# Moving transposes, one block of modulation sums and the first folds of the last norm in a one-core diffusion-layer kernel

## The reference

```python
ada = silu(cond) @ w_ada + b_ada            # six 1024-wide vectors per group
sh1, sc1, g1, sh2, sc2, g2 = split(ada, 6)
h = modulate(layer_norm(x), sh1, sc1)
proj = h @ w_in                             # pooling input, q, k, v, o, gates
pool_out = pool_mixer(proj[..., :512])
ml_out, state = mlstm_mixer(q, k, v, o, gates)   # conv + silu on q,k; chunked scan both ways
mix = concat([pool_out, ml_out]) @ w_out
x = layer_norm(ALPHA * x + g1 * mix, ln1_g, ln1_b)
h = modulate(layer_norm(x), sh2, sc2)
up = h @ w_up; a, g = split(up, 2)          # 2 x 2816 wide
ffn = (gelu(dwconv3x3(g) + b_dw) * a) @ w_down
x = layer_norm(ALPHA * x + g2 * ffn, ln2_g, ln2_b)
```

## Time and profile before

| what | us |
|---|---|
| median of 3 runs | 1347.56 (1346.4 to 1351.62) |
| the profiled execution | 1355.02 |
| its span on the core | 1353.3 |
| PE busy | 1272.9 |
| DVE busy | 1027.4 |
| POOL busy | 668.6 |
| ACT busy | 590.7 |

### The profile page before, as it was taken

The page is one execution under the profiler, slowest core; times in us unless marked ns, Lnnn a source line. Parts: engine busy times, 40 slices in busy tenths (PEclk is TensorE's granted clock), DMA queues, the critical chain, the costliest instruction groups (busy, mean ns, idle before and its releaser), DMA issues.

```text
span 1353.3 us, 21780 instructions
## 1 busy us (share of the span) xinstructions
PE 1272.9 (94%) x7739; PEld 1176.0 (87%) x7739; DVE 1027.4 (76%) x1510; ACT 590.7 (44%) x1023; POOL 668.6 (49%) x505
## 2 busy tenths in 40 slices
PE   5899999989998898998999999999999999999995
PEld 3689999989997776888899999999999988888884
DVE  7565559984567678779988778877785689888698
ACT  5442224345345725445444444544443456345420
POOL 1000999643243111217978888797877874200011
PEclk9899999998999998999999999999999999999998
DMA  9522331473335432111534363535443579946674
GB/s 338 155 78 79 90 88 47 123 234 86 91 104 188 147 120 93 63 63 31 164 131 173 121 205 128 185 117 186 164 152 112 194 249 340 359 138 194 236 258 190
DMA packets 164851, 210.28 MB, mean 155 GB/s; under 512 B 10567, under 2 KB 102819, under 8 KB 164515
## 3 DMA queue, kind: packets, MB, share of 16 engines
q1 hardware_dynamic: 164286, 204.47, 45.7%
q0 software_dynamic: 288, 4.72, 0.9%
q10 hardware_dynamic: 197, 0.06, 0.0%
HBM read 161.49 MB, written 47.72 MB: 155 GB/s over the span
## 4 chain that ended last, share of the span: by engine, by line
PE 79%; DVE 10%; DMA 3%; ACT 3%; issue 3%; POOL 3%; SPq 0%; DVEq 0%; ACTq 0%; POOLq 0%
PE ps L1233 12%; PE ps L1582 11%; PE ps L1580 11%; PE ps L1581 11%; PE ps L1613 5%; PE ps L1614 5%; PE ps L1615 5%; PE ps L1185 2%; PE ps L1456 2%; PE ps L1458 2%; PE ps L1457 2%; DMA adaw<-in_w_ada 2%; DVE qk L2703 1%; PE ps L1511 1%; DVE aacc_side L2723 1%
## 5 line engine op out<-in xcount | busy, mean ns | idle before, releaser
L3038 DVE SCALAR_TENSOR_TENSOR ps<-gs,taps,ps 128x945 f32<-128x945 f32 (+2 forms) x176 | 215.9, 1227 | 57.1 <-ACT ps L1996 51.6
L2361 POOL TENSOR_TENSOR rstd<-mv,neghalf 128x1 f32<-128x1 f32 x27 | 26.0, 963 | 268.5 <-DVE mv L3206 161.5
L1233 PE MATMUL ps<-h1hi,whi 128*128 128x384 f32 x432 | 154.7, 358 | 4.1 <-DVE wlo L2558 3.0
L1233 PE MATMUL ps<-h1hi,wlo 128*128 128x384 f32 x432 | 146.9, 340 | 0.0
L1233 PE MATMUL ps<-h1lo,whi 128*128 128x384 f32 x432 | 146.9, 340 | 0.0
L1613 PE MATMUL ps<-dwhi,uhi 128*128 128x512 f32 x290 | 113.1, 390 | 1.3 <-POOL dwlo L2218 1.3
L1615 PE MATMUL ps<-dwhi,ulo 128*128 128x512 f32 x290 | 112.9, 389 | 0.0
L1614 PE MATMUL ps<-dwlo,uhi 128*128 128x512 f32 x290 | 112.8, 389 | 0.0
L2218 POOL TENSOR_TENSOR wlo<-raw,whi 128x512 fp32r<-128x512 f32 x46 | 68.0, 1480 | 72.7 <-ACT whi L1685 34.5
L1580 PE MATMUL ps<-thi,xhi 128*128 128x288 f32 x320 | 95.0, 297 | 3.3 <-POOL xlo L2218 3.1
L1582 PE MATMUL ps<-thi,xlo 128*128 128x288 f32 x320 | 95.0, 297 | 0.0
(11 more groups left out here) (430 smaller groups left out, 4007.7 us busy)
## 6 DMA issues: line engine op xcount, KB each, us to landing
raw<-in_w_up SPq DMA_DIRECT2D x78, 256.0 KB, 3.9
u_rows<-val SPq DMA_DIRECT2D x22, 576.0 KB, 2.9
adaw<-in_w_ada SPq DMA_DIRECT2D x24, 512.0 KB, 4.1
st<-in_w_down SPq DMA_DIRECT2D x22, 512.0 KB, 4.3
t_rows<-st SPq DMA_DIRECT2D x11, 1024.0 KB, 5.0
raw<-in_w_in SPq DMA_DIRECT2D x40, 256.0 KB, 4.4
w_raw<-in_w_down SPq DMA_DIRECT2D x33, 256.0 KB, 4.6
v_raw<-u_rows SPq DMA_DIRECT2D x33, 256.0 KB, 4.5
```

Of the source, the lines that this page charges most:

```text
L1233: last = mm(ps[:, bank, 0:GN], a[:, n % 2, k * P:(k + 1) * P], b[:, kk, grp(g)], start=(kk == 0 and a is whi and b is h1hi), stop=(kk == K ...
L3038: step(stt(a3[:, ro, co], g3[:, ri, ci], taps[:, tap:tap + 1], a3[:, ro, co], ALU.mult, ALU.add), 2 + m)
```

## The change

The change has four parts. (1) One of the eight first blocks of `w_ada` is loaded ahead of the first two projection weights. (2) One `ada_unit` moves from unit 23 to unit 30; `ada2_cols(5)` leaves unit 31 and stands behind the first matmul group of o-unit 33, directly ahead of the scores; on DVE the last `conv` stands ahead of `ada_evac`. (3) `y_at` has other slots: the transposes of tiles 0, 1, 2, 3, 4, 5, 6 stand at (3,7), (3,13), (4,10), (5,9), (6,8), (7,7), (8,5) in place of (3,12), (4,1), (4,5), (5,5), (6,5), (7,5), (8,5). (4) `N_TAIL` goes from 4 to 8. The second half rows of the last norm are no longer summed first and then gated, scaled and added: `ahead(i)`, in `D_S4` and the start of `D_S3`, gates the partial sum that is there and adds the residual; `fold(i)` gates the missing term, adds it and takes the statistics. The four loads of residual rows for indices 5 to 8 move from `D_U4` to `D_S4` and `D_S3`, and ACT's copies of the `D_S3` banks stand behind unit 6 and not unit 4.

```diff
 KD = KF * 7
 ARING = 4
 N_POOL_LO = 4
-N_TAIL = 4
+N_TAIL = 8
 N_SPLIT = 8
 UX = UC + P
 
@@ -94,7 +94,7 @@
 
 ADA_FIRST = 8
 ADA_UNITS = {4: 2, 6: 2, 7: 1, 8: 1, 9: 2, 10: 1, 11: 1, 12: 1, 13: 1, 14: 1, 15: 1, 16: 1, 17: 1, 18: 1, 19: 1, 21: 2,
-             23: 2, 24: 3, 25: 3, 26: 3, 27: 3, 28: 3, 29: 3}
+             23: 1, 24: 3, 25: 3, 26: 3, 27: 3, 28: 3, 29: 3, 30: 1}
 ADA_SIDE = (3, 5)
 
 
@@ -716,11 +716,11 @@
 
             for t in range(NT):
                 load_x0(t)
-            for i in range(3):
+            for i in range(4):
                 load_ada1(i)
             load_proj(0)
             load_proj(1)
-            for i in range(3, N_LOAD1):
+            for i in range(4, N_LOAD1):
                 load_ada1(i)
             load_proj(2)
             load_proj(3)
@@ -1019,6 +1019,10 @@
             def load_z(i):
                 sp.dma_start(zt[(i - 1) % 4 if i else 4][:, :], x1_rows[TILE_OF[i]]
                              ).then_inc(y_in[(i - 1) % 4] if i else ln_in, 16)
+
+            def load_z_again(i):
+                sp.wait_ge(z_added, ZA_0 + i)
+                load_z(H + i)
 
             def store_y(i):
                 t = TILE_OF[i]
@@ -1070,8 +1074,12 @@
                 load_d(D_S4, j)
                 if j == 5:
                     store_y(0)
+                if j in (6, 8, 10):
+                    load_z_again(j // 2 - 2)
             for j in range(N_SPLIT):
                 load_w(D_S3, j)
+                if j == 1:
+                    load_z_again(4)
                 if j < KF - N_SPLIT:
                     load_w(D_S3, N_SPLIT + j)
                 elif j < KF - N_SPLIT + ARING:
@@ -1083,10 +1091,6 @@
                     load_u(D_U4, j + ARING)
                 if 3 <= j < 3 + KF - N_SPLIT:
                     load_w(D_U4, N_SPLIT + j - 3)
-                if j in (2, 4, 6, 8):
-                    i = j // 2
-                    sp.wait_ge(z_added, ZA_0 + i)
-                    load_z(4 + i)
             for i in range(1, NT - 1):
                 store_y(i)
             for half in range(2):
@@ -1315,6 +1319,7 @@
                 o_unit(U_C, g)
             o_groups = [(n, g) for n in range(U_C + 1, U_OUT) for g in range(NG)]
             o_unit(*o_groups.pop(0))
+            ada2_cols(N_ADA2 - 1)
 
             def scores(s, d):
                 ck = scan_chunks(s)[d]
@@ -1485,7 +1490,7 @@
                     pe.wait_ge(hT_used, NT)
                     pe.wait_ge(n_ready, 1)
                     gate_bcast(1, 6)
-            y_at = {(3, 12): 0, (4, 1): 1, **{(i, 5): i - 2 for i in range(4, NT)}}
+            y_at = {(3, 7): 0, (3, 13): 1, (4, 10): 2, (5, 9): 3, (6, 8): 4, (7, 7): 5, (8, 5): 6}
             for i in range(2, NT):
                 if i == 2:
                     pe.wait_ge(growT_ready, 1)
@@ -2074,7 +2079,7 @@
                 else:
                     act.wait_ge(pe_unit, U_DOWN + KF * (p + 1))
                 if p == D_S3:
-                    act.wait_ge(down_used, 2 + i + 1)
+                    act.wait_ge(down_used, 6 + i + 1)
                 fn(z[i][:, UC:DM] if p == D_S1 else z[i][:, 0:UC], ps[:, BANKS[SET[p]][i], :], ACT.Copy).then_inc(p_copied, 1)
 
             def t_split(b, n):
@@ -2200,7 +2205,7 @@
             for j in range(KF):
                 both_hi(D_S3, j)
             for j in range(KF):
-                if j == 4:
+                if j == 6:
                     for i in range(H):
                         copy_at_end(D_S3, i)
                 both_hi(D_U4, j)
@@ -2761,10 +2766,10 @@
                     ada_unit(unit)
                 if n % 2 == 0 and n // 2 > 2 * H:
                     conv(n // 2 - 1 - 2 * H)
+            conv(2 * H - 1)
             dve.wait_ge(pe_ada, N_ADA1 + N_ADA2)
             link(ada_evac(6, A_G1, A_G2))
             tsc(ada1p[:, 1, :, :], adaT[:, A_SC2:A_SC2 + KT, :], 1.0, None, ALU.add).then_inc(ada_b, 1)
-            conv(2 * H - 1)
             dve.wait_ge(pool_y, 4)
             v.tensor_copy(Cs[:, :, :, P:P + 1], colv[:, V_N:V_N + 2 * H].rearrange("p (d h n) -> p d h n", d=2, n=1)
                           ).then_inc(cs_n, 1)
@@ -3160,16 +3165,33 @@
                 dve.wait_ge(p_copied, PC_0 + 2 + i + 1)
                 tt(z[H + i][:, 0:UC], z[i][:, 0:UC], ps[:, BANKS[1][i], :], ALU.add).then_inc(down_used, 1)
 
-            def c12(i):
-                dve.wait_ge(pe_unit, U_DOWN + KF * (D_S4 + 1))
-                dve.wait_ge(p_copied, PC_0 + 8 + i + 1)
-                out = z[H + i][:, UC:DM]
-                tt(out, out, ps[:, BANKS[1][i], :], ALU.add).then_inc(down_used, 1)
-
-            def c22(i):
-                dve.wait_ge(p_copied, PC_0 + 16 + i + 1)
-                out = z[i][:, UC:DM]
-                tt(out, out, z[i][:, 0:UC], ALU.add).then_inc(down_used, 1)
+            def ahead(i):
+
+                t, cols = TILE_OF[i], slice(UC, DM)
+                out = z[t][:, cols]
+                dve.wait_ge(p_copied, PC_0 + 8 + i)
+                link(tt(out, out, grows2[:, who(t), cols], ALU.mult))
+                dve.wait_ge(y_in[(i - 1) % 4], 16 * (times((i - 1) % 4) + (i - 1) // 4 + 1))
+                ins = stt(out, zt[(i - 1) % 4][:, cols], ALPHA, out, ALU.mult, ALU.add)
+                if i < 5:
+                    ins.then_inc(z_added, 1)
+                    dve.wait_ge(z_added, ZA_0 + i)
+                else:
+                    link(ins)
+
+            def fold(i):
+
+                t, slot, cols = TILE_OF[i], (2 * NT + i) % 4, slice(UC, DM)
+                out, gate, term = z[t][:, cols], grows2[:, who(t), cols], z[(i - 1) % 4][:, 0:UC]
+                if i < 5:
+                    dve.wait_ge(pe_unit, U_DOWN + KF * (D_S4 + 1))
+                    link(tt(term, ps[:, BANKS[1][i - 1], :], gate, ALU.mult))
+                else:
+                    dve.wait_ge(p_copied, PC_0 + 16 + i - 4)
+                    link(tt(term, term, gate, ALU.mult))
+                tt(out, out, term, ALU.add).then_inc(down_used, 1)
+                dve.wait_ge(down_used, 6 + i)
+                link(v.bn_stats(stats[:, slot, 6:12], out))
 
             def part(i, half):
 
@@ -3182,22 +3204,14 @@
                     dve.wait_ge(down_used, half + 1)
                     link(tt(out, out, gate, ALU.mult))
                 elif i < 5:
-                    dve.wait_ge(down_used, (6 if half else 2) + i)
-                    link(tt(out, out, gate, ALU.mult))
-                elif half:
-                    dve.wait_ge(down_used, 10 + i - 4)
+                    dve.wait_ge(down_used, 2 + i)
                     link(tt(out, out, gate, ALU.mult))
                 else:
                     dve.wait_ge(pe_zt, N_ZT + 8 + i - 4)
                     link(tt(out, ps[:, BANKS[0][t], :], gate, ALU.mult))
                 if i:
                     dve.wait_ge(y_in[(i - 1) % 4], 16 * (times((i - 1) % 4) + (i - 1) // 4 + 1))
-                ins = stt(out, zt[(i - 1) % 4 if i else 4][:, cols], ALPHA, out, ALU.mult, ALU.add)
-                if 0 < i < 5 and half:
-                    ins.then_inc(z_added, 1)
-                    dve.wait_ge(z_added, ZA_0 + i)
-                else:
-                    link(ins)
+                link(stt(out, zt[(i - 1) % 4 if i else 4][:, cols], ALPHA, out, ALU.mult, ALU.add))
                 link(v.bn_stats(stats[:, slot, 6 * half:6 * half + 6], out))
 
             def spread(i):
@@ -3262,35 +3276,26 @@
                 s3(j)
                 if j == 0:
                     part(4, 0)
+                if j in (1, 3, 5, 7):
+                    ahead((j + 1) // 2)
             for j in range(KF):
                 both_lo(D_S3, j)
-                if j >= 7:
-                    c12(j - 7)
-                if j == 7:
-                    part(1, 1)
-                    spread(1)
-                if j == 8:
-                    part(2, 1)
-                    spread(2)
-                if j == 9:
-                    gain(1)
-                if j == 10:
-                    part(3, 1)
-                    spread(3)
+                if j < H:
+                    ahead(5 + j)
+                if j in (7, 8):
+                    fold(j - 6)
+                    spread(j - 6)
             for j in range(KF):
                 both_lo(D_U4, j)
-                if j == 0:
-                    gain(2)
-                if j == 1:
-                    part(4, 1)
-                    spread(4)
-                if j == 2:
-                    gain(3)
-                if j == 4:
-                    gain(4)
-                if j >= 7:
-                    c22(j - 7)
-                    part(j - 2, 1)
+                if j in (0, 2):
+                    fold(3 + j // 2)
+                    spread(3 + j // 2)
+                if 3 <= j < 7:
+                    gain(j - 2)
+                if j == 8:
+                    fold(5)
+            for i in range(6, NT):
+                fold(i)
             part(5, 0)
             spread(5)
             part(6, 0)
```

## The result

| | before | after |
|---|---|---|
| median, us | 1348.37 (6 runs, 1346.4 to 1352.51) | 1338.72 (6 runs, 1337.12 to 1339.68) |
| profiled execution, us | 1355.02 | 1337.12 |
| its span, us | 1353.3 | 1335.4 |

The ratio is 0.9903 with a 95% interval of 0.9885 to 0.9921: 9.65 us faster between the medians, where 11.3 were forecast. The changed kernel was timed twice more beside the experiments: 0.9934 [0.9915, 0.9953] and 0.9925 [0.9901, 0.995].

The account below looks back on a forecast made before the run. PE was taken to bound the kernel (busy 1272.9 of 1353.3 us), with DVE setting the end. 0 − 1.2 − 5.5 − 4.6 = −11.3 from 1347.56 gave 1336.3 us, range 1332 to 1343.

Parts of the forecast that it names:

- Load order, 0: First loads: one block and the two weights behind it trade places; counted as 0, ±0.3 us.
- The scan's entry, −1.2: Scan's entry: PE waits of 4.0 us go, numerators 3.0 us earlier, low clock after new idle charged 1.8; net −1.2.
- The rule of the Trainium skill: Scan's entry: waits between matmul groups drop PE to half speed; by it +2.9 us, 1340.4, chance 0.12.
- the bad end: Scan's entry, unfavourable end: full clock loss of 4.6 and loads at 6.3 us, so 2.9 us lost.
- The transposes, −5.5: Output projection: the 6.09 us wait for `tb` goes, against about 1.5 new; DVE's chain ends 5.5 us earlier.
- its end of −7: Output projection, favourable end: 6.09 us plus half the clock loss, less the new 1.5.
- The four thin margins: Output projection: `tb` 2, 3, 4, 7 ready 0.3 to 0.7 us before PE; one missed gives 1341.8, chance 0.10.
- The tail, −4.6: Behind the last matmul: DVE ends 8.0 us after it, at 1346.2 instead of 1350.84; −4.6 us.
- the rival of the late unit: Last products: operands of unit 10 come too late, PE stalls 5.8 us, giving 1342.1; chance 0.10.
- The sum: Whole kernel: 0 − 1.2 − 5.5 − 4.6 = −11.3 us; forecast chance 0.48.

Follow-up runs that it names:

- no_load: The changed kernel with the old order of the first loads (part 1 undone): 1339.39 us, ratio 0.9898 to the kernel before.
- full_again: The changed kernel timed and profiled once more, unaltered: 1341.36 us, ratio 0.9934 to the kernel before.
- no_transposes: The changed kernel with the old places of the transposes (part 3 undone): 1346.63 us, ratio 0.9968 to the kernel before.
- no_sums: The changed kernel with the old sums, fold and convolution order at the scan's entry (part 2 undone): 1340.53 us, ratio 0.9916 to the kernel before.
- first_earlier: The changed kernel with only the first tile's transposes at the new place, all others at the old ones: 1343.46 us, ratio 0.995 to the kernel before.
- no_tail: The changed kernel with the old tail, four units tile by tile (part 4 undone): 1344.53 us, ratio 0.995 to the kernel before.
- full_third: The changed kernel once more, unaltered, as measure for three other runs on the same chip: 1341.71 us, ratio 0.9925 to the kernel before.

## Why the prediction was right

The forecast was 1336.3 in a range of 1332 to 1343; 1338.72 was measured, and the sign, the bound and the three places were right. Point by point:

**Load order, 0.** Held as far as can be measured: with the new order PE waits between nothing and 2.8 us for `adaw`, without it 1.6 and 1.7, and `no_load` is no slower (0.9898).

**The scan's entry, −1.2.** The mechanism came as worked out: both waits gone, scores earlier, loads late, idle of 4.3 us (4.2 forecast), lower clock behind it. Scores at 309.29 and numerators at 318.69 were each about 1.5 us earlier than the forecast's 312.3 and 321.7, once the 1.5 us are taken off by which this trace was ahead at the 1401st matmul. The low clock lasted 3.4 us in this profile, as in most of the others with the idle, and cost 1.7 (1.8 forecast), not the 4.6 that the old waits had cost; in `full_again` and `no_transposes` it lasted 6.8 us. Against `no_sums` the part is worth 0.9 to 1.6 us, against the profile of before 2.6 to 3.3, since that one had the longer cold stretch (10.2 us; `no_sums` 6.8). The rule of the Trainium skill on waits between groups ("TensorE: Matmul & The Clock Gate", section "HAM oscillation — how this bites in real kernels") showed in its direction, and the part gained nonetheless: the trace's 1.7 us decides. What I didn't see was that another place for the fold would give 6.0 us more. One slip in the working: for the bad end the loads were put 1.3 us later, where 6.3 less the 5.3 of the forecast is 1.0; that gives an end of 2.6 lost and not 2.9.

**The transposes, −5.5.** By the stage −7.3 like with like, by the times −6.3 (−5.3 against the one run beside it). So by the stage the term is 1.8 too small and just beyond its end of −7. What was mis-sized is the clock: I had part of its loss eaten by DVE, but the wait of 6.1 and the 3.4 us lost in the 6.8 us cold stretch behind it went whole, against new waits of 1.4 and 0.7 us, and 6.1 + 3.4 − 2.1 = 7.4. One sentence was wrong: the transposes at 522.85 are those of the third tile, not "The second tile's"; the second's stand at 512.93 without a wait. The argument rests on the third's residual add anyway, but the wrong name hid the part of the second tile's place (`first_earlier`). The four thin margins held: no wait for `tb` but the last tile's 1.4 us (1.5 forecast). DVE's five waits for PE are gone, all of the 4.4 us and not 3.4.

**The tail, −4.6.** 15.42 − 10.86 = 4.6 in the stage, 3.9 by the times; DVE's last instruction ends 8.0 us behind the last matmul, as forecast. DVE had 14 instructions and 8.7 us more in `D_S4`, where I had counted 8 and 5.8; PE did not wait for it. The operands came in time, so the rival of the late unit fell. `D_S4` moved 283 GB/s (281 forecast); `D_S3` moved 315, not 249, and `D_U4` 159, against 280 before; it fits that loads came forward which SP had issued in `D_U4`, but I did not count them.

**The sum.** −11.3 against −9.65, with an uncertainty of ±2.5. Over the three comparisons the changed kernel's 18 runs have a median of 1339.8 and the 30 of the kernel before 1350.6: −10.8. The parts undone one by one add up to more, 0.9 to 1.6, 7.3 and 4.6 in the stages, 12.8 to 13.5 in all; that the times give 2 to 3 us less is within their intervals and is not explained. The mechanisms are the ones forecast; that the sum lies so near is in part luck, since the transposes' term was too small and the kernel before timed 3 us faster in the runs that the forecast started from (1347.56) than in all 30.

## What to carry to other kernels

A wait that is taken away by moving its instruction later can show up again at whoever waits for that instruction. Here SP's loads of the next stage did wait, for 4.3 us of idle on PE and a clock drop; a place shortly behind the point at which the result is ready was worth 6.0 us more than the late one. When two changes each remove one limit of the same stretch, try them together. The new folds alone shortened the tail by nothing and the pass of eight units alone lost 4.3 us against `no_tail`; together they gained 3.9 to 4.6. The first tile's earlier transposes alone gave 0.8 us, the later ones 4.0, all together 7.3. And read the places in a list by counting, not by the order in which waits appear.

## What the runs showed of the hardware that I had not expected

Executions of one kernel spread over 10.8 us: 1333.68 to 1344.45 for 18 of the changed kernel, and the six of `full_third`, all on one chip, already over 10.5. The time follows the mean granted clock that each execution lists, 0.977 to 0.986, with a correlation of −0.82 and a slope of 9 us per 0.01; for 24 of the kernel before it is −0.78 and 8 us. In the profiles these are stretches of 3.4 us, or a few times that, at 1.2 GHz; a few come behind the same wait in every profile, others (in the projection and early in the feed-forward) in one profile and not in the next. A stretch of 3.4 us costs 1.7 us where PE is the bound (1.1 us in the output projection, by the table), so one pair of profiles can misjudge a change by several us, as the first pair here did with 17.9 for some 11.
